# Softmax scaled on VectorE before the transposes, instead of after the value product

## The reference, cut to what matters

```
m     = max(max(logits), sink)
p     = exp(logits - m)
denom = sum(p) + exp(sink - m)
out   = (p / denom) @ v
```

## Time and profile before

| | |
|---|---|
| median of three runs | 1493.11 us |
| the profiled execution, its own time | 1494.01 us |
| its span, first to last instruction | 1492.2 us |
| TensorE matmul busy | 1431.8 us (96%) |
| VectorE busy | 867.6 us (58%) |
| ScalarE busy | 617.9 us (41%) |
| mean granted TensorE clock | 0.990 of full speed |
| first attention | about 151 to 223 us |
| second attention | about 769 to 943 us |

### The profile page before, as it was taken

One profiled execution on the slowest core, in us unless ns is written; L12 is line 12 of the kernel. 1 busy time (PEld: TensorE's weight loads), 2 busy tenths in 40 slices (PEclk: granted clock), 3 DMA queues, 4 the chain that ended last, 5 costly groups with the idle time before them and its releaser, 6 DMA issues.

```text
span 1492.2 us, 17741 instructions
## 1 busy us (share of the span) xinstructions
PE 1431.8 (96%) x7272; PEld 1153.7 (77%) x7272; DVE 867.6 (58%) x1221; ACT 617.9 (41%) x985; POOL 1.9 (0%) x7
## 2 busy tenths in 40 slices
PE   6999999999999999999998999989799999999997
PEld 5877778788788888887876677767588888888885
DVE  7887654647545353555667676488754443453445
ACT  5453653433313122233346667777533221231232
POOL 0000000000000000000000000000000000000000
PEclk9999999999999999999999999999999999999999
DMA  4222214231323233232221111222222322323222
GB/s 162 85 86 86 71 57 139 87 101 62 101 98 99 86 99 112 85 99 85 72 73 54 58 43 63 80 71 85 76 94 85 99 99 92 99 92 107 91 91 107
DMA packets 36561, 131.64 MB, mean 88 GB/s; under 512 B 4432, under 2 KB 4560, under 8 KB 36224
## 3 DMA queue, kind: packets, MB, share of 16 engines
q1 hardware_dynamic: 36128, 127.16, 26.2%
q0 software_dynamic: 352, 3.34, 0.6%
HBM read 128.39 MB, written 2.10 MB: 87 GB/s over the span
## 4 chain that ended last, share of the span: by engine, by line
PE 74%; DVE 15%; ACT 8%; issue 2%; DMA 1%; SPq 0%; DVEq 0%; ACTq 0%
PE gp L1434 21%; PE gp L1436 20%; PE gp L1435 20%; DVE w_lo L833 2%; ACT arena L589 2%; ACT w_hi L438 1%; DVE arena L1083 1%; DVE arena L1076 1%; PE mp L1637 1%; PE gp L1510 1%; PE mp L1647 1%; PE gp L1512 1%; PE gp L1511 1%; DVE arena L1338 1%; DVE arena L1339 1%
## 5 line engine op out<-in xcount | busy, mean ns | idle before, releaser
L1434 PE MATMUL gp<-h_hi,w_hi 128*128 128x512 f32 x944 | 373.5, 396 | 19.7 <-ACT arena L724 11.9
L1435 PE MATMUL gp<-h_lo,w_hi 128*128 128x512 f32 x944 | 370.1, 392 | 0.0
L1436 PE MATMUL gp<-h_hi,w_lo 128*128 128x512 f32 x944 | 369.8, 392 | 0.0
L833 DVE TENSOR_TENSOR w_lo<-raw,w_hi 128x1024 fp32r<-128x1024 f32 x232 | 283.3, 1223 | 144.4 <-ACT w_hi L438 143.4
L438 ACT ACTIVATE w_hi<-raw 128x1024 fp32r<-128x1024 f32 x232 | 243.0, 1051 | 160.9 <-PE gp L1436 104.8
L1434 PE MATMUL gp<-a_hi,w_hi 128*128 128x512 f32 x704 | 276.5, 393 | 1.4 <-DVE w_lo L833 1.1
L1436 PE MATMUL gp<-a_hi,w_lo 128*128 128x512 f32 x704 | 274.0, 389 | 0.0
L1435 PE MATMUL gp<-a_lo,w_hi 128*128 128x512 f32 x704 | 274.0, 389 | 0.0
L1434 PEld LDWEIGHTS gp<-h_hi,w_hi 128*128 128x128 f32 x944 | 178.8, 189 | 63.2 <-issue 22.0
L1436 PEld LDWEIGHTS gp<-h_hi,w_lo 128*128 128x128 f32 x944 | 178.9, 190 | 37.9
L1435 PEld LDWEIGHTS gp<-h_lo,w_hi 128*128 128x128 f32 x944 | 179.0, 190 | 36.6
(11 more groups left out here) (255 smaller groups left out, 1509.0 us busy)
## 6 DMA issues: line engine op xcount, KB each, us to landing
raw<-slabs SPq DMA_DIRECT2D x232, 512.0 KB, 3.5
arena<-x_in SPq DMA_DIRECT2D x4, 512.0 KB, 6.3
arena<-x_in POOLq DMA_DIRECT2D x1, 2048.0 KB, 8.9
out_t<-arena SPq DMA_DIRECT2D x8, 256.0 KB, 2.2
arena<-bias POOLq DMA_DIRECT2D x1, 1024.0 KB, 5.2
arena<-s5b SPq DMA_DIRECT2D x1, 512.0 KB, 8.5
arena<-s5c SPq DMA_DIRECT2D x1, 512.0 KB, 9.2
par<-params SPq DMA_DIRECT2D x1, 232.0 KB, 2.7
```

The costliest lines, as they stand in the source:

```text
L833: TT(w_lo[:, n % RING, :], raw[:, n % RAW, :], w_hi[:, n % RING, :].bitcast(F32), ALU.subtract).then_inc(w_lo_ready, 1)
L1434: pe.matmul(dst, hi, x_hi(t), start=t == 0, stop=False)
L1435: pe.matmul(dst, hi, x_lo(t), start=False, stop=False)
L1436: ins = pe.matmul(dst, lo, x_hi(t), start=False, stop=t == tiles - 1)
```

## The change

The probabilities are divided by their sums before they are transposed, on VectorE, where a query is a partition and the inverse sum a scalar of the partition. `outputs` on VectorE and `spread_inverse` on TensorE go. TensorE now waits for the scaled probabilities, where it waited for the exponentials. What ScalarE takes from PSUM is the finished output; in `att1` it writes it as the high part at once, and VectorE forms the low part from PSUM. TensorE's value product waits for those reads of the unit before, because it writes the same PSUM bank. On VectorE `scaled_probs(u+1)` stands before `logits(u+2)`, and at the head of the loop `inverse_sums(0)` and `scaled_probs(0)` stand before `logits(1)`. `z_low` comes one iteration earlier.

```diff
                 def take_outputs(u):
                     act.wait_ge(at_done, A.u0 + u + 1)
-                    nc.scalar.activation(A.of_heads(A.q, u), by_heads(mp[:, 5, 0:2 * P]), ACT.Copy).then_inc(at_copied, 1)
-
-                def outputs_hi(u):
-                    act.wait_ge(at_read, A.u0 + u + 1)
-                    nc.scalar.activation(A.of_heads(h_hi, u), A.of_heads(A.q, u), ACT.Copy).then_inc(h_hi_ready, 1)
+                    o = by_heads(mp[:, 5, 0:2 * P])
+                    if A.name:
+                        nc.scalar.activation(A.of_heads(h_hi, u), o, ACT.Copy).then_inc(h_hi_ready, 1)
+                    else:
+                        nc.scalar.activation(A.of_heads(A.q, u), o, ACT.Copy).then_inc(at_copied, 1)
...
-                def outputs(u):
-                    o = A.of_heads(A.q, u)
-                    dve.wait_ge(at_copied, A.u0 + u + 1)
-                    TT(o, o, by_heads(mp[:, 5, 2 * P:4 * P]), ALU.mult).then_inc(at_read, 1)
+                def scaled_probs(u):
+                    L = A.logit[u % 2]
+                    lo, hi = A.span(u)
+                    dve.wait_ge(inv_ready, A.u0 + u + 1)
+                    for h in range(4):
+                        ins = TS(L[:, h, lo:hi], L[:, h, lo:hi], mini[u % 3][:, 5, h:h + 1], None, ALU.mult)
+                        if h < 3:
+                            V.up(ins)
+                    ins.then_inc(probs_ready, 1)
...
                 logits(0)
+                inverse_sums(0)
+                scaled_probs(0)
                 logits(1)
-                inverse_sums(0)
                 between(0)
                 for u in range(n):
                     if u + 1 < n:
                         inverse_sums(u + 1)
-                    if u:
-                        outputs(u - 1)
-                    if u + 2 < n:
-                        logits(u + 2)
                     if A.name and u:
                         outputs_low(u - 1)
                     if u + 1 < n:
+                        scaled_probs(u + 1)
+                    if u + 2 < n:
+                        logits(u + 2)
+                    if u + 1 < n:
                         between(u + 1)
...
-                def spread_inverse(u):
-
-                    pe.wait_ge(inv_ready, A.u0 + u + 1)
-                    if A.u0 + u:
-                        pe.wait_ge(at_read, A.u0 + u)
-                    for h in range(2):
-                        for p in range(2):
-                            lane = mini[u % 3][:, 5, 2 * p + h:2 * p + h + 1]
-                            pe.matmul(mp[HD * p:HD * p + HD, 5, (2 + h) * P:(3 + h) * P], lane.to_broadcast([P, HD]), ident,
-                                      start=True, stop=True, skip_group_check=True)
...
-                    pe.wait_ge(ex_done, A.u0 + u + 1)
+                    pe.wait_ge(probs_ready, A.u0 + u + 1)
...
-                    spread_inverse(u)
+                    if u:
+                        pe.wait_ge(*((h_lo_ready, H_AT["y1"] + u) if A.name else (at_copied, u)))
```

More of the change, by code:

```diff
@@ L262, in build @@
         inv_ready, pt_done, pt_ready = sem("inverse_sums"), sem("probs_transposed"), sem("probs_t_ready")
+        probs_ready = sem("probs_scaled")
         at_done, at_copied = sem("attention_done"), sem("attention_copied")
         glu_sig = sem("glu_sigmoid")
-        at_read = sem("attention_read")
         lg_done, lru_sig, lru_tanh, lru_act, lru_root, lru_free = (
@@ L611, in attention @@
                         nc.scalar.activation(A.pt[:, j, :], mp[:, 3 + g % 2, :], ACT.Copy).then_inc(pt_ready, 1)
-                    if A.name and u:
-                        outputs_hi(u - 1)
                     if u + 1 < n:
@@ L621, in attention @@
                 if A.name:
-                    outputs_hi(n - 1)
                     z_chunk(CT - 1)
@@ L1093, in inverse_sums @@
                     dve.reciprocal(row[:, 5, :], row[:, 5, :]).then_inc(inv_ready, 1)
-                def outputs(u):
-                    o = A.of_heads(A.q, u)
-                    dve.wait_ge(at_copied, A.u0 + u + 1)
-                    TT(o, o, by_heads(mp[:, 5, 2 * P:4 * P]), ALU.mult).then_inc(at_read, 1)
+                def scaled_probs(u):
[7 more added lines that the diff above has]
+                    ins.then_inc(probs_ready, 1)
                 def outputs_low(u):
                     dve.wait_ge(h_hi_ready, H_AT["y1"] + u + 1)
-                    TT(A.of_heads(h_lo, u), A.of_heads(A.q, u), A.of_heads(h_hi, u).bitcast(F32),
+                    TT(A.of_heads(h_lo, u), by_heads(mp[:, 5, 0:2 * P]), A.of_heads(h_hi, u).bitcast(F32),
                        ALU.subtract).then_inc(h_lo_ready, 1)
@@ L1119, in attention @@
                     if u + 1 < n:
+                        scaled_probs(u + 1)
+                    if u + 2 < n:
+                        logits(u + 2)
+                    if u + 1 < n:
                         between(u + 1)
-                outputs(n - 1)
                 if A.name:
@@ L1131, in gate_slab @@
                 split(SLAB["gate_s"] + AHEAD + u)
-                if u == 2:
+                if u == 1:
                     z_low(CT - 2)
@@ L1317, in _ @@
             attention(att2, inputs2)
-            dve.wait_ge(at_read, att2.u0 + len(att2.units))
+            dve.wait_ge(at_copied, len(att2.units))
             ahead = itertools.count(SLAB["mix"] + AHEAD)
@@ L1741, in recurrence_gates @@
                         pe.wait_ge(a_lo_ready, A_AT["uc"] + DC)
-                        pe.wait_ge(at_read, att2.u0 + len(att2.units))
+                        pe.wait_ge(at_copied, len(att2.units))
                     t, cols = o // 4, slice(q * P, (q + 1) * P)
```

## The result

The changed kernel takes 1499.76 us (median of 6 runs, 1498.68 to 1501.19), the kernel before beside it 1493.08 us (6 runs): a ratio of 1.0044, 95% interval 1.0031 to 1.0057. Measured once more, beside other variants, it took 1497.78 us against 1493.61 us: 1.0027, interval 1.0016 to 1.0038. The profiled execution took 1500.02 us, its span is 1498.2 us.

A forecast was written before the change was run, and what follows sets the result against it. TensorE was taken to bound the first attention, a ring of VectorE and ScalarE the second. -2.5 (first) + 4.9 (second) + 1.5 (clock) = +3.9 us: 1497.9 us profiled, 1497.0 us as median; range 1491.5 to 1501.0 us.

The forecast's parts named there:

- a ring of VectorE and ScalarE: Second attention, 384-key units: exponentials, slab take, convolution, inverse sums, logits close in 10.89 us without TensorE.
- The rival that wanted this idle time used: Scaling fits VectorE's idle time in the convolution half, TensorE sets the pace everywhere: about -11 us, 1482 us; chance 0.12.
- the opening: Start of an attention: +2.05 us in the second, up to unit 5; 0.85 us lost at the first's third slab.
- The price of the scaling: VectorE's time for one scaling instruction within SBUF: 420 ns for 384 elements, 353 ns for 256.
- the two halves: Second attention's unit pair, 384 keys: the half with the convolution grows 1.15 us, the half without it nothing.
- The second attention without the clock, +4.9: Second attention: +7.5 us on the ring by unit 14, less 1.2 us slack and 1.5 us for three spreads.
- the four halves: Second attention, convolution halves of 384 keys ahead of units 6, 8, 10 and 12: +4.6 us together.
- unit 14: Second attention, the convolution half of 256 keys ahead of unit 14: +0.9 us.
- given back at the end: Second attention's end, TensorE the bound again: 1.2 us of slack and 1.5 us for three spreads less.
- The clock, +1.5: TensorE's longer waits ahead of the third chunk, second attention: clock falls to 1.2 GHz twice in four, 0.75 us each.
- The first attention, -2.5: First attention, TensorE the bound: spreads gone gives -3.4 us, the opening loses 0.85 us, net -2.5 us.
- the spreads: TensorE's spread matmuls of the inverse sums, first attention: 0.49 us a unit on the path, -3.4 us in all.

The follow-up runs named there:

- the scaling behind the logits: Changed kernel with VectorE's order alone altered in both attentions: logits of unit u+2 before inverse sums and scaling of unit u+1; 1483.07 us, ratio 0.9933.
- the scaling's work twice: Changed kernel with four more multiplications by one per chosen unit, second attention: behind the convolution 1508.39 us, in the twin's other half 1501.23 us.
- the second profile: Changed kernel run again with nothing altered: profiled execution 1499.56 us, span 1497.8 us; median 1497.78 us, ratio 1.0027.
- the kernel that has only this part: Change made in the first attention alone, the second spreading inverse sums on TensorE as in the kernel before; 1491.46 us, ratio 0.9989.

## Why the prediction was right, step by step

Forecast +3.9 us against the profiled execution, 1497.0 us as a median; measured +6.0 us, 1499.76 and, the second time, 1497.78 us. The mechanism held, and so did the side. Of the sizes one met its number by luck, and the chances of the clock are as large as the terms that were missed.

- **The bound.** That the second attention runs on a ring of VectorE and ScalarE, in spite of TensorE's 96%, is shown by the scaling behind the logits (10.30 us) and by the scaling's work twice (13.69 us against 12.03, of which the added set is 1.45 and the clock 0.2). The rival that wanted this idle time used was priced at 1482 us; the kernel that uses it takes 1483.07 us. That its price came so near is luck in part: it took TensorE to set the pace everywhere, and in that kernel TensorE still waits 0.81 to 1.09 us ahead of the third chunk, while 4.4 us come from the opening.
- **The price of the scaling.** 420 and 353 ns were taken, 416 and 348 measured. Its placement in the two halves: +1.15 and nothing were taken, +1.14 and nothing measured, where the clock had not fallen.
- **The second attention without the clock, +4.9.** Its parts: the four halves 4.55 for 4.6 (the fall's 0.2 us taken out); unit 14, 0.87 for 0.9; given back at the end 2.4 for 2.7; the opening, from the first exponentials to unit 5, 1.26 for 2.05. Together +4.3. In the second profile the opening measured 1.83 us, the rest the same: +4.8. The two openings differ by 0.56 us between units 3 and 4 alone, and there by the clock: behind a wait of 5.54 us the slow matmuls last from 792.35 to 796.75 us in the first profile, 4.4 us, and from 794.14 to 799.39 in the second, 5.3 us (5.7 in the kernel before). So the opening was mis-sized by 0.2 us, and the rest of its shortfall is one execution's chance.
- **The clock, +1.5.** In the profiled execution 0.2 + 1.6 = 1.8 us, from two falls in four waits, as forecast. The sum is luck: I had put 0.75 on each, and it is 0.2 to 0.5 inside the ring and 1.6 at its end. In the second profile two falls cost 0.2 + 0.5 = 0.7 us. How many waits trip it, and which, differs between executions of one program: after 3.25 and 2.81 us of idle in the second profile, after 3.27 and 2.18 in the first. The Trainium skill (TensorE: Matmul & The Clock Gate, Part 1) says that the check runs free of the kernel; these two profiles agree, as the wait of 2.80 us left the clock up in the first and the same one of 2.81 us brought it down in the second.
- **The first attention, -2.5.** This is the step that failed in size: -1.8 us, both from the last value product (221.79 to 220.01) and from the kernel that has only this part. A unit gained 0.44 us, where 0.49 was taken, the distance from the spread's start to the value product's: the spreads gave 3.06 us for 3.4. And the opening lost 1.28 us for 0.85.
- **Not foreseen: +1.7 us behind the second attention** in the profiled execution, which the second profile doesn't have, so it is not the change's. About 1.3 us of it are the slow sums and spread at the end; the other 0.4 us lie before 1483 us, and where is not shown.

Sum of the profiled execution: -1.8 + 4.3 + 1.8 + 1.7 = +6.0 us. Of the second, by span: -1.8, +1.8 for a fall near 690 us (last section), +5.5 in the second attention (4.8 and 0.7), nothing behind it: +5.6 us with rounding. What of this is the change's is better told by the two ratios, 1.0044 and 1.0027: +4 to +6.5 us.

## What to carry to other kernels

Before work is moved to an engine with spare time, find out where its idle time lies in its queue: 2 us of idle ahead of an instruction don't cover work that stands behind it. When two engines pass a unit back and forth, write the ring down with its times; if it closes without the busiest engine, that engine's relief is worth nothing while it does, and the first edit to try is the order of the others: here the same instructions cost 4 to 7 us in one place and come with 10 us of gain in another. Work on data that is needed a whole unit later belongs behind the work that the next engine waits for.

## What the runs showed of the hardware

The same program loses 1 to 2 us in single executions at waits of TensorE that the kernel before has too. The clearest is the wait at the column sums near 688 us, 1.31 us long in every kernel. First profile of the changed kernel:

```profile
688.30 1.05 PE L1459 MATMUL mp<-par,arena 128*128 128x1 f32 x8 [1.31 <-DVE arena L844]
...
690.00:700.00 10.00, 8.92 (x43) 6.61 (x42) 6.10 (x9) 3.70 (x6) 0.00 (x0) 1.00 0.16 54
```

and the second, each with its stretch of 10 us behind:

```profile
688.19 1.05 PE L1459 MATMUL mp<-par,arena 128*128 128x1 f32 x8 [1.31 <-DVE arena L844]
...
690.00:700.00 10.00, 9.74 (x35) 7.80 (x34) 4.34 (x7) 3.09 (x5) 0.00 (x0) 0.66 0.10 40
```

From 690 to 700 us the granted clock is 1.00 in the first and 0.66 in the second, and there the second profile's lead turned into 1.8 us of lag (first exponentials of the second attention at 773.83 and 772.05 us). There the slow matmuls start some 2 us behind the wait's end, at 690.34. So the clock came down behind waits of 1.3 and 2.0 us, and not behind others of 2.8 and 3.1 us (1052.75 in the earlier trace rows). A comparison of two single profiles of such a kernel can't tell 2 us; the pitch of a repeated unit can tell far less, since the undisturbed halves agree to 0.01 us in three profiles and the disturbed ones to 0.05.
